# Splitting 544 tokens as 296 + 248, and feeding the second part's high and low rows through one 496-column matmul

## The reference: what is computed

```python
a_in, a_gate, u, v, q, k, vv, g = split(x @ w_in)            # 1024 -> 6656 columns
y_a = silu(layer_norm(causal_dwconv(a_in * sigmoid(a_gate))))  # width 31
y_b = gelu(u) * spatial_gate(layer_norm(gelu(v)))
y_c = stick_breaking_attention(q, k, vv)
merged = sum(sigmoid(g_i + b_i) * (y_i @ w_branch[i]))
x = layer_norm(ALPHA * x + merged @ w_out)                   # "out": 1024 x 1024
f_gate, f_val = split(x @ w_up)                              # "up": 1024 x 5632
f = gelu(causal_dwconv(f_gate)) * f_val                      # width 3
x = layer_norm(ALPHA * x + f @ w_down)                       # "down": 2816 x 1024
```

## Time and profile before

| | |
|---|---|
| median of three runs | 1821.95 us |
| profiled execution, its own time | 1822.0 us |
| its span | 1820.3 us |
| PE busy | 1804.0 us, 99% of the span |
| PEld busy | 1761.1 us, 97% |
| DVE busy | 1135.1 us, 62% |
| ACT busy | 771.5 us, 42% |
| PE's share of the chain that ended last | 95% |

### The profile page before, as it was taken

How to read it: one execution, slowest core, us unless ns; L and a number is a source line. 1 busy time by engine, 2 the same in 40 slices (tenths; PEclk the granted TensorE clock), 3 DMA queues, 4 the chain that set the end, 5 groups by cost and what they waited for, 6 DMA issues and landing times.

```text
span 1820.3 us, 32909 instructions
## 1 busy us (share of the span) xinstructions
PE 1804.0 (99%) x14362; PEld 1761.1 (97%) x14362; DVE 1135.1 (62%) x1737; ACT 771.5 (42%) x1220; POOL 88.9 (5%) x159
## 2 busy tenths in 40 slices
PE   9999999999999999999999999999999999999997
PEld 9998899999999999999999889999999999999997
DVE  5788677654764444446668886676557644445565
ACT  4245432353553444434542564333544544434343
POOL 0024000000100000000000340000001000000000
PEclk9999999999999999999999999999999999999999
DMA  4521122222222222255525211222232222223544
GB/s 169 190 95 48 36 95 70 82 93 93 95 83 78 93 93 94 68 182 174 170 85 190 75 67 36 72 88 87 82 128 70 72 91 93 93 79 99 182 160 134
DMA packets 36512, 186.02 MB, mean 102 GB/s; under 512 B 7376, under 2 KB 11728, under 8 KB 18192
## 3 DMA queue, kind: packets, MB, share of 16 engines
q1 hardware_dynamic: 34960, 178.37, 29.0%
q10 hardware_dynamic: 1408, 5.54, 0.8%
HBM read 176.75 MB, written 7.15 MB: 101 GB/s over the span
## 4 chain that ended last, share of the span: by engine, by line
PE 95%; DVE 3%; ACT 1%; DMA 1%; issue 0%; ACTq 0%; DVEq 0%
PE acc L1628 29%; PE acc L1633 28%; PE acc L1634 28%; PE score L1702 1%; DVE wl L961 1%; PE small L1750 1%; PE turned L1729 1%; ACT wh L495 1%; DMA raw<-wdn 1%; PE score L1633 1%; PE score L1634 1%; PE score L1628 1%; PE small L1762 1%; PE turned L1786 0%; PE score L1904 0%
## 5 line engine op out<-in xcount | busy, mean ns | idle before, releaser
L1628 PE MATMUL acc<-xh,wh 128*128 128x272 f32 x2944 | 858.7, 292 | 2.5 <-DVE xl L915 1.5
L1633 PE MATMUL acc<-xl,wh 128*128 128x272 f32 x2944 | 848.5, 288 | 0.0
L1634 PE MATMUL acc<-xh,wl 128*128 128x272 f32 x2944 | 847.5, 288 | 0.0
L1628 PEld LDWEIGHTS acc<-xh,wh 128*128 128x128 f32 x2944 | 555.3, 189 | 18.1 <-issue 13.1
L1633 PEld LDWEIGHTS acc<-xl,wh 128*128 128x128 f32 x2944 | 555.0, 189 | 0.1
L1634 PEld LDWEIGHTS acc<-xh,wl 128*128 128x128 f32 x2944 | 553.9, 188 | 0.0
L961 DVE TENSOR_TENSOR wl<-raw,wh 128x2048 fp32r<-128x2048 f32 (+2 forms) x154 | 318.4, 2068 | 204.1 <-ACT wh L495 203.3
L495 ACT ACTIVATE wh<-raw 128x2048 fp32r<-128x2048 f32 (+2 forms) x174 | 304.9, 1753 | 158.9 <-DMA raw<-wdn 112.1
L1628 PE MATMUL acc<-fhh,wh 128*128 128x272 f32 x704 | 204.9, 291 | 1.9 <-DVE wl L961 1.8
L1634 PE MATMUL acc<-fhh,wl 128*128 128x272 f32 x704 | 202.6, 288 | 0.0
L1633 PE MATMUL acc<-fll,wh 128*128 128x272 f32 x704 | 202.6, 288 | 0.0
(11 more groups left out here) (256 smaller groups left out, 2255.8 us busy)
## 6 DMA issues: line engine op xcount, KB each, us to landing
raw<-win SPq DMA_DIRECT2D x50, 1024.0 KB, 4.9
raw<-wup SPq DMA_DIRECT2D x44, 1024.0 KB, 4.9
raw<-wdn SPq DMA_DIRECT2D x32, 1024.0 KB, 4.9
raw<-wbr SPq DMA_DIRECT2D x24, 512.0 KB, 3.6
raw<-wdn SPq DMA_DIRECT2D x16, 768.0 KB, 4.2
raw<-wout SPq DMA_DIRECT2D x8, 1024.0 KB, 4.9
v_out<-vfm ACTq DMA_DIRECT2D x2, 1088.0 KB, 9.4
k_out<-k ACTq DMA_DIRECT2D x2, 1088.0 KB, 4.7
```

Of the source, the lines that this page charges most:

```text
L1628: first = mm(out, a, xs[0], start=start, stop=False)
L1633: mm(out, a, xs[1], start=False, stop=False)
L1634: return mm(out, b, xs[0], start=False, stop=stop)
```

## The change

The parts are now N0 = 296 and N1 = 248 columns (PART), everywhere in the kernel; tiles for one part are WIDE = 296 columns wide. The high and low rows of each source lie in one tile with two planes (`xx`, `mm_`, `ff`, and likewise `ybb`, `ycc`, `yaa`). In the out, up and down stages, for h = 1, one matmul with `wh` takes the 248 high columns and the 248 low columns as one moving operand of 496 columns and writes 496 columns of the bank: wh·xh in the first 248, wh·xl in the next. The matmul with `wl` (248 columns) adds to the first 248. The two halves of the bank are then added by VectorE. The last tile of the last `down` keeps three matmuls. All other units keep three matmuls, of 296 or 248 columns.

```diff
-HALF = T // 2
-BP = SEQ - HALF
+N0, N1 = 296, 248
+PART = (N0, N1)
+WIDE = max(PART)
+BP = SEQ - N0
...
-            def three(out, s, at, xs, start, stop):
+            def three(bank, s, at, xs, t, h, start, stop, wide=False):
                 a, b = wh[s][:, at:at + P], wl[s][:, at:at + P]
-                first = mm(out, a, xs[0], start=start, stop=False)
+                n = PART[h]
+                cols = dcol(h) if xs[0].shape[-1] == T else slice(0, n)
+
+                def by_high(part, **flags):
+                    if wide:
+                        return mm(bank[:, 0:2 * N1].rearrange("p (a n) -> p a n", a=2), a, xs[2][:, :, t, cols], **flags)
+                    return mm(bank[:, 0:n], a, xs[part][:, t, cols], **flags)
+
+                def by_low(**flags):
+                    return mm(bank[:, 0:n], b, xs[0][:, t, cols], **flags)
+
+                if wide and not start:
+                    first = by_low(start=False, stop=False)
+                else:
+                    first = by_high(0, start=start, stop=False)
...
-                mm(out, a, xs[1], start=False, stop=False)
-                return mm(out, b, xs[0], start=False, stop=stop)
+                if wide:
+                    return by_low(start=False, stop=False) if start else by_high(0, start=False, stop=stop)
+                by_high(1, start=False, stop=False)
+                return by_low(start=False, stop=stop)
```

VectorE's and ScalarE's new work, for each tile of h = 1 in those stages:

```diff
+            def add_tile(x, b, h, wide):
+                dve.wait_ge(acc_full[b], c.take(acc_full[b]))
+                ins = v.tensor_tensor(x, x, ps[b][:, 0:PART[h]], ALU.add)
+                if wide:
+                    ins.then_inc(vec, c.up(vec))
+                    dve.wait_ge(vec, c.seen(vec))
+                    ins = v.tensor_tensor(x, x, ps[b][:, N1:2 * N1], ALU.add)
+                ins.then_inc(acc_free[b], c.up(acc_free[b]))
...
-                def residual(t, b, h):
+                def residual(t, b, h, wide=False):
...
+                    if wide:
+                        ins.then_inc(vec, c.up(vec))
+                        dve.wait_ge(vec, c.seen(vec))
+                        ins = v.tensor_tensor(x, x, ps[b][:, N1:2 * N1], ALU.add)
...
+                def gate_sums(banks=ps):
+                    skip((0, 1))
+                    for b in (2, 3):
+                        m, bank = b % 2, banks[b]
+                        c.skip(acc_full[b])
+                        dve.wait_ge(low_rows, c.take(low_rows))
+                        rows = gex[:, m, 2 + N0:2 + SEQ]
+                        v.tensor_tensor(rows, rows, bank[:, 0:BP], ALU.add).then_inc(vec, c.up(vec))
+                        rows = gex[:, m, 4 + SEQ:GEX]
+                        v.tensor_tensor(rows, rows, bank[:, BP:N1], ALU.add).then_inc(acc_free[b], c.up(acc_free[b]))
```

ScalarE's gate copies for banks 2 and 3 now read the low halves (`bank[:, N1:...]`) and signal `low_rows`. For the value banks 2 and 3 ScalarE first copies the low half to `tmp`; VectorE adds the high half to it and then multiplies by the gelu, and only then can ScalarE round:

```diff
                 def f_rows(i, b):
                     c.skip(acc_full[b])
-                    act.wait_ge(acc_free[b], c.take(acc_free[b]))
-                    A(row(fhh[b // 2], 2 * i + b % 2, 0, HALF), tmp[:, b, :], ACT.Copy).then_inc(f_hi, c.up(f_hi))
+                    c.skip(acc_free[b])
+                    if b < 2:
+                        act.wait_ge(acc_free[b], c.seen(acc_free[b]))
+                    else:
+                        if b == 2 and i:
+                            act.wait_ge(f_ready, c.take(f_ready, 4))
+                        act.wait_ge(acc_full[b], c.seen(acc_full[b]))
+                        A(tmp[:, b, 0:N1], (FIRST_VALUE if i == 0 else ps)[b][:, N1:2 * N1], ACT.Copy).then_inc(
+                            low_rows, c.up(low_rows))
+                        act.wait_ge(f_made, c.take(f_made))
+                    A(fhh[b // 2][:, 2 * i + b % 2, :], tmp[:, b, 0:PART[b // 2]], ACT.Copy).then_inc(f_hi, c.up(f_hi))
...
-                down(0, shift)
-                down(1, moments)
-                down(1, shift)
+                down(0, lambda: shift(0))
+                down(1, lambda: moments(0))
+                down(1, lambda: shift(1), last=r == DEPTH - 1)
```

More of the change, by code:

```diff
@@ L1031, in last_tiles @@
                 for b in range(4):
[L1032 to L1034 removed]
+                    add_tile(x[:, 4 + b], b, h, wide)
                     if b == 1 and between:
@@ L1648, in unit @@
                         each(t)
-                    last = three((spare or ps[b])[:, 0:HALF], s, t * 256 + m * P, [x[:, t, dcol(b // 2 if h is None else h)] for x in xs],
-                                 t == 0, t == nk - 1)
+                    last = three(spare or ps[b], s, t * 256 + m * P, xs, t, part, t == 0, t == nk - 1,
+                                 wide and part == 1)
                     if mid and t == nk // 2 - 1:
@@ L1655, in unit, with chunk @@
                     read.append(s)
-            def chunk(xs=(xh, xl), nk=KT, first=None, mid=None, end=None):
+            def chunk(xs=(xh, xl, xx), nk=KT, wide=False, first=None, mid=None, end=None):
                 s = arrived()
@@ L1929, in _ @@
                     chunk()
-                    chunk(xs=ya, nk=CT, first=ya_tiles if i == 0 else None)
+                    chunk(xs=(*ya, yaa), nk=CT, first=ya_tiles if i == 0 else None)
                 ss = []
@@ L1938, in _ @@
                             ss.append(arrived())
-                        unit(ss[t // 2], t % 4, t % 2, (mh, ml), KT, m_tiles if t == 0 else None, h=h,
-                             done=h == 1 and t % 2 == 1)
+                        unit(ss[t // 2], t % 4, t % 2, (mh, ml, mm_), KT, m_tiles if t == 0 else None, h=h,
+                             done=h == 1 and t % 2 == 1, wide=True)
                         if t == 5:
-                            shift()
+                            shift(h)
                         if h == 1 and t == 0:
                             turn_bank()
-                            moments()
+                            moments(0)
                 gone = [c.seen(acc_free[b]) for b in range(4)]
@@ L1959, in _, with down @@
                     unit(s0, 2 + m, m, xs, KT, arrive(1) if m == 0 else None, h=1, spare=bs[m],
-                         free=(acc_free[m], gone[m] + 1), done=m == 1)
+                         free=(acc_free[m], gone[m] + 1), done=m == 1, wide=True)
                 for m in range(2):
-                    unit(s1, 2 + m, m, xs, KT, h=1, spare=FIRST_VALUE[2 + m], done=m == 1)
+                    unit(s1, 2 + m, m, xs, KT, h=1, spare=FIRST_VALUE[2 + m], done=m == 1, wide=True)
                 for m in range(2):
                     unit(s2, 2 + m, m, xs, KT, h=1, spare=SECOND_GATE[2 + m],
-                         free=(acc_free[2 + m], gone[2 + m] + 1), done=m == 1)
-                chunk()
-                for r in range(9):
-                    chunk()
-                    chunk()
-                def down(h, middle=None):
+                         free=(acc_free[2 + m], gone[2 + m] + 1), done=m == 1, wide=True)
+                chunk(wide=True)
+                for _ in range(9):
+                    chunk(wide=True)
+                    chunk(wide=True)
+                def down(h, middle=None, last=False):
                     at = 0
```

339 lines of the change are left out of this document (178 added, 161 removed).

## The result

The changed kernel takes 1847.13 us (median, 1845.53 to 1848.17), the kernel before 1822.15: a ratio of 1.0135, 95% interval 1.0117 to 1.0153. The forecast was 1828.0 with a range to 1838. The direction was right, the size was not: 25 us slower, not 6.

The account below looks back on a forecast made before the run. The prediction took PE, the matmul engine, to bound the kernel: 1822.0 us, less 1.4 for removed matmuls, plus 3.6 behind out, 1.4 at the layer's end and 2.4 in the downs, gives 1828.0 us, range 1808 to 1838.

Parts of the forecast that it names:

- Column price: PE's matmuls: 0.450 to 0.458 ns a column, not 0.417, so 496 columns take about 227 ns and no columns are saved.
- Rival (1): PE: the 12 ns belong to the matmul, columns cost 0.417 ns, 13.9 us go, total 1816.6 us; chance 0.13.
- rival (2): PE: 272 and 296 columns share a floor of 125.3 ns, 496 cost 208.7, 48 us go, total 1783.5; chance 0.07.
- a wide matmul that is nearly free: PE: 512 columns take about 131 ns in a stream of loads and matmuls, some 114 us less; 1 in 100.
- 1.2 ns a matmul: PE in out, up and down: each of 1162 removed matmuls saves 1.2 ns, 1.4 us in all (0 to 3.4).
- In the stages that keep three matmuls ... nothing: Stages without the wide matmul: sum over both parts stays the same, only the order of long and short differs, no cost.
- Moments behind out, +1.8: Out to up: VectorE's two-step adds delay the sums PE awaits, 1.8 us of new stall, twice, 3.6 us (2 to 5).
- The four residual adds ahead of the shift, held by 3 us: Out, h = 1, ahead of the shift: 3 us of idle VectorE cover the added work, so no cost.
- Down to the next layer, +1.4: Layer's end, once: VectorE's last sum comes later than PE needs it, 1.4 us more (0 to 2.5).
- Downs, +2.4: Second-part downs: late weights and a later split at the third-to-fourth turn, 1.2 us a layer, 2.4 us (0 to 6).
- Up, "cost at nothing": Up stage: added copies and adds, about 2 us VectorE and 1 us ScalarE per chunk pair, cost nothing on half-busy engines.
- Rival (4): Up: ScalarE waits for VectorE's products before rounding weights, PE waits 1 us in half of 44 chunks, 1850 us; chance 0.05.

Follow-up runs that it names:

- the split alone: Kernel before with parts of 296 and 248, three matmuls for both parts everywhere and the consumers of before: 1829.98 us, ratio 1.0051.
- after: The changed kernel whole, and its trace, against the kernel before: 1847.13 us, ratio 1.0135.
- the kernel with the fillers: Changed kernel plus 16 unneeded matmuls of 248 columns behind the first up unit, ahead of the moments, once a layer: 1844.97 us, ratio 1.0130.
- down only: Kernel with parts of 296 and 248, three matmuls elsewhere, and the wide matmul in the down projection only: 1834.51 us.
- both first: Changed kernel; in the first up pair VectorE's weight split precedes the second part's products and ScalarE's first two gate copies precede its rounding of them: 1840.09 us.
- the steady kernel with 296 and 248: Kernel before, parts of 272, except 19 steady up chunks a layer in parts of 296 and 248 with the wide matmul: 1821.03 us, ratio 0.9995.

## Why the prediction failed, step by step

The price of a column and the chains at the moments and at the layer's end were forecast well, and the gain of a removed matmul was put too low. What failed is the cover: work added to VectorE and ScalarE in up was put at nothing because both engines are half free, the residual adds ahead of the shift were held to be covered, the downs' waits were mis-sized, stages with three matmuls were put at nothing, and the clock had no term. These five steps are 2.4 us in the forecast, all of them the downs', and 24.7 us in the sum below.

- **Column price: right.** Next to nothing is saved on columns: 496 take 224 to 226 ns from start to start, 296 take 136 to 137, 248 take 114 to 115. Rival (1), which needs 219, and rival (2), which needs 209, fell by that, and so did a wide matmul that is nearly free. The Trainium skill's rule for a warm matmul by itself ("TensorE: Matmul & The Clock Gate", Back-to-back issue gap), N/2.4 + 2.5 ns, has 209 ns for 496 columns; this trace has 15 to 17 more, and the trace decides.
- **"1.2 ns a matmul": mis-sized.** It is 6.7 ns a removed matmul in the up pairs, of which the uneven split takes 2.1 back. Its bounds, 0 to 2.9, came from differences of record lengths, whose ends are modelled, and a few ns of error in them are all of this term. In up alone the net is 704 x 4.6 = 3.2 us, where the forecast has 1.4 for all stages: an error to the good.
- **"In the stages that keep three matmuls ... nothing": wrong.** The shorter second part ends sooner, and the weights that follow it come late: four waits in the conv stage are 0.74 us instead of 0.41, 1.3 us together, and the split alone, without one wide matmul, costs 9 us.
- **Moments behind out, +1.8: right.** The gap grew from 0.58 to 2.32 us in layer 0, 1.7. In after the first of its two parts is:

```profile
509.96 0.30 PE L1702 MATMUL score<-xx,wl 128*128 128x296 f32 x1
511.97 0.69 PE L1753 MATMUL small<-st,mean_d 128*128 128x248 f32 x2 [1.71 <-DVE st L1080]
```

- **The four residual adds ahead of the shift, held by 3 us: wrong**; 1.27 and 0.94 us of stall. The idle 3.05 us were counted to the operation that the shift releases. VectorE's sum was there 2.4 us ahead of PE (495.96 to 498.35); against that stand 1.8 us of adds, PE's six short units ahead of the shift (6 x 0.28 = 1.7 us less time, which the step left out) and the norm of the wider part. In after the sum comes late:

```profile
499.46 1.37 DVE L1032 TENSOR_TENSOR st<-pair 128x248 f32<-128x248 f32 x1
501.61 1.19 DVE L1039 SCALAR_TENSOR_TENSOR xT<-xT,small 128x992 f32<-128x992 f32 x1 [0.78 <-PE small L1749]
```

- **Down to the next layer, +1.4: right** (1.43, from no gap; 0.99 to 1.43 in the variants).
- **Downs, +2.4: too small.** Stalls in the downs are 10.4 us against 2.3 before, 8.1 more, over the range's 6. I priced one chunk for its weights and one turn; each second-part down waits (1.2, 1.5), and at the turn the norm's whole chain, 9% wider, stands before the shorter down.
- **Up, "cost at nothing": the step that failed most.** Half-free engines say nothing of order. The first pair has 3.14 us of stall, twice, and with the fall of the clock behind each that is 9.7 us for a term of 0 (3.4 of it are among the clock's 6.8 us below). Rival (4) had this mechanism, weights behind the products, but as a mean over 44 chunks; it happened in one chunk a layer and not at all in the steady ones. The experiments show the mechanism: with both queues reordered there the stall was gone in both layers, with one of them it stayed.
- **The clock: no term at all.** Four more stretches at 1.2 GHz cost some 6.8 us. The earlier trace rows showed such a stretch before the change, read there for its column price alone.

The terms as measured, against before: -3.2 for PE's matmuls in up, 3.5 for the moments, 2.2 for the shift, 1.4 at the layer's end, 8.1 in the downs, 6.3 in the first pairs, 1.3 in four waits for weights of the conv stage (0.74 for 0.41 us each), 6.8 for the clock. That is 26.4, for 25.1 between the spans; what PE saves in out and down isn't in it, since no stretch there gives a period. By the 6.7 ns of up the 458 matmuls that go there would be 3.1 us, an estimate; 1.3 us is what the sum lacks.

## What to carry to other kernels

Where an edit gives an engine more work in steps that wait for another engine, walk its queue at each place where the steady rhythm begins, turns or ends, and ask what stands behind the new waits; a busy share below a half covers a steady loop and nothing else. If a bound engine waits for two things that end close together, the profile names one, and mending one shows the other. Then put the gain only where it is free: here 19 steady chunks a layer took most of the gain in up (1.6 of 1.7 to 2.1 us a layer) and nearly none of the loss. And where the clock falls in some runs and not in others, a trace or two do not show what brought it: compare many runs.

## What the runs showed of the hardware

- A stall of TensorE often costs more than its length: behind most of the stalls of 1.9 to 3.2 us, 30 of 38 in twelve traces, the granted clock was 0.50 for 3.4 us, up to 1.7 us more. It is not certain: behind the same stall of 1.91 us it fell in one run and not in another of the same kernel, behind the 3.14 us of the first up pairs it fell in after and not in the kernel with the fillers, and behind 2.86 us at the turn it fell in five traces and not in down only's. Where sixteen useless matmuls stood in the wait it did not fall, but neither did it without them in one run of both first.
- Such stretches came without any long stall too, at 210 to 218 and at 1109 to 1130 us, in the same place of both layers, where PE was doing matmuls of 32 columns for the decoder's rows; in before at 1109.4. Each of the 13 in eleven of the seventeen traces began between the first of these matmuls and 1.2 us behind the last; the other six traces have the same matmuls and no such fall. PE in the steady kernel with 296 and 248, where its fall of 1111.3 us begins:

```profile
1110.62 0.65 PE L1881 MATMUL small<-att,vc 128*64 128x32 f32 x8
1111.20 0.37 PE L1883 MATMUL small<-att,vtok 32*64 32x32 f32 x2
```
- The same number of columns in parts of 296 and 248 took PE 0.07 us more for 192 matmuls than in parts of 272. No run here shows why.
- A matmul that fills a bank's 512 columns takes 228 to 230 ns, in line with the 224 to 226 for 496.
